# Projection products two behind each chunk stage, instead of spread over all 48 stages

## Time and profile before

| | |
|---|---|
| median of 3 runs | 2930.36 us (2925.32 to 2940.78) |
| profiled execution | 2926.02 us, span 2924.5 us |
| TensorE busy | 2652.7 us (91%) |
| VectorE busy | 993.6 us (34%) |
| ScalarE busy | 656.7 us (22%) |
| mean granted TensorE clock | 0.933 of full speed |

### The profile page before, as it was taken

How to read it: one execution, slowest core, us unless ns; L and a number is a source line. 1 busy time by engine, 2 the same in 40 slices (tenths; PEclk the granted TensorE clock), 3 DMA queues, 4 the chain that set the end, 5 groups by cost and what they waited for, 6 DMA issues and landing times.

```text
span 2924.5 us, 44189 instructions
## 1 busy us (share of the span) xinstructions
PE 2652.7 (91%) x18133; PEld 2145.4 (73%) x18133; DVE 993.6 (34%) x1760; ACT 656.7 (22%) x1033; POOL 19.1 (1%) x26
## 2 busy tenths in 40 slices
PE   5989888888999999999999999954969999999997
PEld 3656565665767676767767676744969999999997
DVE  1111111114536362635454453545142221222222
ACT  2221121212122222222231312130133221112111
POOL 0000000000000000000000000010000000000000
PEclk9989898989999998999999999957989999999999
DMA  3010101010000000000000000002001111111112
GB/s 130 26 60 14 59 14 59 14 46 1 31 2 31 1 32 1 2 31 2 31 2 31 2 31 2 30 16 115 29 28 44 45 47 45 50 43 50 39 49 78
DMA packets 22394, 99.57 MB, mean 34 GB/s; under 512 B 4912, under 2 KB 5104, under 8 KB 19328
## 3 DMA queue, kind: packets, MB, share of 16 engines
q1 hardware_dynamic: 20640, 88.45, 8.6%
q0 software_dynamic: 1632, 9.21, 0.9%
HBM read 86.31 MB, written 11.34 MB: 33 GB/s over the span
## 4 chain that ended last, share of the span: by engine, by line
PE 86%; DVE 9%; issue 3%; ACT 2%; DMA 0%; DVEq 0%; SPq 0%; ACTq 0%
PE banks L531 86%; ACT arena L899 1%; DVE arena L1479 1%; DVE arena L1487 0%; DVE arena L1488 0%; DMA arena<-in_consts 0%; DVE arena L1470 0%; DVE arena L1469 0%; DVE arena L1321 0%; DVE arena L1323 0%; DVE arena L1490 0%; DVE arena L1481 0%; DVE arena L1234 0%; DVE arena L1644 0%; ACT L899 0%
## 5 line engine op out<-in xcount | busy, mean ns | idle before, releaser
L531 PE MATMUL banks<-arena 64*64 64x64 f32 (+9 forms) x12770 | 1805.8, 317 | 226.8 <-DVE arena L1597 58.1
L531 PEld LDWEIGHTS banks<-arena 64*64 64x64 f32 (+1 forms) x12770 | 1299.0, 171 | 731.8 <-issue 411.4
L531 PE MATMUL banks<-merged_high,gate_up_high 128*128 128x344 f32 x1056 | 338.6, 321 | 23.6 <-DVE gate_up_low L1628 23.6
L531 PE MATMUL banks<-x_low,gate_up_high 128*128 128x344 f32 x1056 | 338.0, 320 | 0.0
L531 PE MATMUL banks<-merged_high,gate_up_low 128*128 128x344 f32 x1056 | 337.8, 320 | 0.0
L899 ACT ACTIVATE arena<-arena 128x64 f32<-128x64 f32 (+7 forms) x289 | 178.2, 634 | 382.4 <-DVE arena L1414 257.0
L1628 DVE TENSOR_TENSOR gate_up_low<-arena,gate_up_high 128x1024 fp32r<-128x1024 f32 (+1 forms) x76 | 82.4, 1085 | 435.7 <-ACT gate_up_high L1152 435.7
L531 PEld LDWEIGHTS banks<-merged_high,gate_up_high 128*128 128x128 f32 x1056 | 198.9, 188 | 24.1 <-issue 24.1
L531 PEld LDWEIGHTS banks<-merged_high,gate_up_low 128*128 128x128 f32 x1056 | 199.1, 188 | 0.0
L531 PEld LDWEIGHTS banks<-x_low,gate_up_high 128*128 128x128 f32 x1056 | 198.9, 188 | 0.0
L531 PE MATMUL banks<-hidden_high,gate_up_high 128*128 128x344 f32 x528 | 169.3, 321 | 0.0
(11 more groups left out here) (149 smaller groups left out, 1407.0 us busy)
## 6 DMA issues: line engine op xcount, KB each, us to landing
arena<-in_w_gu SPq DMA_DIRECT2D x44, 512.0 KB, 3.7
arena<-in_w_pair SPq DMA_DIRECT2D x8, 2112.0 KB, 8.1
arena<-in_w_gla SPq DMA_DIRECT2D x4, 3072.0 KB, 9.7
arena<-in_xT SPq DMA_DIRECT2D x16, 516.0 KB, 6.9
arena<-in_w_d SPq DMA_DIRECT2D x16, 384.0 KB, 3.1
arena<-in_w_d SPq DMA_DIRECT2D x16, 320.0 KB, 2.9
out_yT<-arena SPq DMA_DIRECT2D x8, 516.0 KB, 3.0
arena<-in_gla_s POOLq DMA_DIRECT2D x4, 1024.0 KB, 5.0
```

Of the source, the lines that this page charges most:

```text
L531: return nc.tensor.matmul(out, lhsT, rhs, start=start, stop=stop)
```

## The change

`slot(m)` gives product m a slot. Before, the 75 products are spread evenly over slots 0 to 46, one or two in each. After, two stand in each slot from 0 on, so the 75 fill slots 0 to 36, one stands in 37, and 38 to 47 have none. `ends` follows from it, and with it the slots of the work on ScalarE and VectorE:

    --- before
    +++ after
             SPREAD = len(PRODUCTS) - 6
             def slot(m):
    -            return m * (SLOTS - 1) // SPREAD if m < SPREAD else SLOTS
    +            return m // 2 if m < SPREAD else SLOTS
             ends = {(job, b): slot(m) for m, (job, b, kt, n) in enumerate(PRODUCTS) if kt == n - 1}

The slots of a job's last products, banks 0, 1, 2:

| job | before | after |
|---|---|---|
| W | 0, 0, 1 | 0, 0, 1 |
| A | 1, 2, 3 | 1, 2, 2 |
| K | 8, 13, 18 | 6, 10, 14 |
| R | 23, 28, 33 | 18, 22, 26 |
| N | 33, 34, 35 | 27, 27, 28 |
| V | 40, 45, behind the stages | 32, 36, behind the stages |

So kk moves from slot 40 to 33, the decayed keys from 44 to 37.

More of the change, by code:

```diff
@@ L407, in slot @@
         def slot(m):
-            return m * (SLOTS - 1) // SPREAD if m < SPREAD else SLOTS
+            return m // 2 if m < SPREAD else SLOTS
         ends = {(job, b): slot(m) for m, (job, b, kt, n) in enumerate(PRODUCTS) if kt == n - 1}
```

## The result

The changed kernel takes 2986.2 us (median of 4 runs, 2985.3 to 2989.4) against 2927.8 for the kernel before: a ratio of 1.0195, 95% interval 1.0164 to 1.0226. The profiled execution took 2989.4 us, 63.4 more than that of before.

What follows compares the result with a forecast made beforehand. TensorE was taken to bound the loop passes. To 2926 us came 31 for stalls, hand-overs and pass 0 and 35 for lost clock, less 4 at the head: 2988, by the median 2992, stated as 2990 (2948 to 3050).

Steps and rivals of the forecast that it cites:

- kk, wait for U in slot 35: Slot 35: TensorE waits for the U copy, delayed on VectorE by V's first shift and kk; 0.9 us a pass.
- decayed keys, wait for SS 38: Slot 38: the state update comes late behind V's second shift and the decayed keys; TensorE stalls 1.6 us a pass.
- N to V: Slot 28: V's first product waits until VectorE has bounded N's first block; 0.25 us a pass (0 to 0.5).
- pass 0: First pass, nothing interleaved: kk and keys wait for V's shifts, TensorE waits for the keys; 1 to 1.5 us more.
- hand-overs in the empty tail: Slots 39 to 46: six waits of 0.38 us for VectorE's copies, uncovered by products; 1.5 us a pass (0.75 to 2.3).
- clock, tail less head: Half clock in tail and into transposes, 35 us in all, less 4 us won at the denser pass heads.
- about 2.4: Tail chunks without products: us a chunk at full clock, against 3.48 at half clock.
- +2 to 5: Transposes with V's last six products, starting at half clock: us a pass lost until the clock returns.
- Rival A: The clock holds in the tail, only stalls and hand-overs cost; about 2958 us (2947 to 2967), chance 0.30.
- rival B: The clock falls in the tail and stays low through the Gram products; 3050 us (3020 to 3075), chance 0.17.
- The head: Slots 3 to 8, two products each: the clock returns a little sooner, winning 4 us in all (0 to 15).
- rival C: Not slower: the denser head brings the clock back at once and the tail keeps it; about 2930 us, chance 0.11.

Runs made afterwards that it cites:

- the kernel with four empty slots: Against the kernel before: its even spread shortened to slots 0 to 43, only the last four slots empty; 2933.7 us, ratio 1.0009.
- the side work moved: Against the changed kernel: inverse decays, kk and decayed keys moved to slots 33, 32 and 35, tail left empty; 2952.9 us, ratio to before 1.0075.
- the empty slots apart: Against the changed kernel: still two products a slot, but every fifth slot empty instead of ten at the end; 2942.9 us, ratio to before 1.0044.
- the dense heads: Against the kernel before: three or two products in each of the first slots, old order from slot 35 on; 2922.4 and 2923.6 us.
- the dense head with two: Against the kernel before: two products in each of slots 0 to 11, then one or two, old order from slot 35 on; 2923.6 us, ratio 0.9976.

## Why the prediction held, and where a size was off

The steps, in the prediction's order, with its terms and what the profile of the changed kernel has:

| step | forecast | measured |
|---|---|---|
| kk, wait for U in slot 35 | 0.9 us a pass | 0.9 |
| decayed keys, wait for SS 38 | 1.6 us a pass | 1.8 |
| N to V | 0.25 us a pass | 0.2 |
| pass 0 | 1 to 1.5 us | 2.0 |
| hand-overs in the empty tail | 1.5 us a pass (0.75 to 2.3) | 2.4 |
| clock, tail less head | 31 us in all | 24.2 |
| sum | 62 us | 63.2 |

*The stalls* were right in place and size: VectorE's side work in a fixed order, end to end, against what TensorE has left. Moving that work alone took 20.8 us of idle time away.

*The empty tail* was sized too small. The lower end of its range halved the 2.69 us of TensorE work that a chunk took at half clock. At full clock the chunk alone takes 2.60 us, 1.81 of it TensorE, so the small matmuls do not halve, and the exposed part is 0.75 us a chunk, the upper end. I should have taken the hand-over rows as they stood.

*The clock* fell in all seven tails and was back in the transposes, as forecast and as the last pass suggested. Its price was 7 us less than forecast. A bare chunk at half clock took 3.47 us as forecast, but 2.60 at full clock and not "about 2.4". And the piece behind the last U copy took 9.3 to 10.9 us, where the kernel with four empty slots took, at full clock:

```profile
1182.30 8.12 PE banks L531 x128
```

That is 2.0 us a pass more, the lower end of the "+2 to 5". So the close sum is in part luck: the hand-overs came out 6.3 us above their term and the clock 6.8 below its own.

One reading behind this step was also wrong. The 1.43 us in front of the first pass are a piece of the chain of waits; in order of time TensorE itself stood idle 1.20 us there. The comparison stands: in all eleven profiles the clock held in the first pass, behind idle times of at most 1.4 us, and fell at the head of every pass from 2 to 7, behind 1.5 to 2.2 us. That does not make the length of the wait the cause, and in the tail no such wait is needed: with the side work moved the clock fell behind none above 0.41 us.

Rival A is excluded by the clock of 0.51 in the tail, rival B by 0.98 from 1213 us on. That thin work in a row is the cause, not the stall in front and not the number of products a slot, follows from four runs together: without the stall the fall comes later, with the empty slots apart, and the same hand-overs, it does not come, with full products in them it does not come, with 23 instead of 10 it lasts 23.9 us. What in the thin work loses the clock, its small matmuls or its short gaps, is not separated.

*The head* (rival C, and the 4 us in the sum): the low stretches fell from 81.9 to 71.7 us, half of which is 5.1. Over all profiles, none of the 48 heads with two or three products in the first slots was low for more than 13.7 us, and of the 18 thinner ones five were, for 17.1. That speaks for an effect, but it varies by run: the dense head with two had 81.9 too, so that the 4 us of the forecast came out at 5.1 is partly chance. Whether it explains the steadier times of the dense heads stays open, as only one run of each was profiled.

## What to carry to other kernels

Work that fills another engine's waits is worth most where each wait gets one piece; a second piece behind the same wait covers nothing, and the waits left bare are paid in full. When the filling moves, the side work tied to it moves too: for each long instruction on the helping engine, add up what stands in front of the next copy and compare it with what the filled engine has left. A row of bare waits costs more than its waits, since TensorE can lose its clock in it and carry half clock into the dense work behind; if a plan must have bare slots, spread them.

## What was not expected

Thin filling can be worse than none: 70 extra matmuls of 174 columns, 21 us at full clock (an estimate, half of the 41 of the whole ones), cost 36 us over the empty tail, while 70 of 348 columns cost 5 or less.

In the triangular inverse, where TensorE has no wait inside a stretch of 41 us, the clock was lost in some passes of three of the eleven profiles. The chain of the kernel with the empty slots apart has the stretch at both levels:

```profile
901.40 47.52 PE banks L532 x318
...
1065.50 40.95 PE banks L532 x318
```

and its window in the first of them:

```profile
904.00:918.00 14.00, 14.00 (x59) 12.56 (x59) 4.22 (x6) 0.58 (x1) 0.00 (x0) 0.51 0.00 1
```

The same 318 matmuls took 6.6 us longer; three such stretches lie in that profile, which took 2952.8 us, where the kernel's fastest run took 2938.5. What decides between the two is not shown here.
